# Choosing experts on VectorE: 112 candidate sums for each head in place of 256, in wide operations with one operand in PSUM

## The chip, the cores and the metric

The kernel runs on one core of a Trainium2 chip. The metric is the device time of one execution in microseconds (us), as the median of several runs. A profile of one execution stands beside it.

## The reference, cut to what matters

The reference is a two-part model of two layers each over 256 tokens of width 1024. The change lies in the second part, in the feed-forward of product-key experts (`peer_ffn`), once for each of the two layers. For every token and each of 8 heads it finds the 16 best of 128 keys in each of two halves, adds every value of the one half to every value of the other, and takes the 16 best of these 256 sums. The place of each of the 16 tells which two keys make the expert:

```python
scores = jnp.einsum('thcd,hcnd->thcn', q, sub_keys)
sv, si = lax.top_k(scores, PEER_TOPK)                      # 16 of 128, for two halves
cand_s = (sv[:, :, 0, :, None] + sv[:, :, 1, None, :]).reshape(t, PEER_HEADS, 256)
cand_i = (si[:, :, 0, :, None] * PEER_NKEYS + si[:, :, 1, None, :]).reshape(t, PEER_HEADS, 256)
best_s, best_p = lax.top_k(cand_s, PEER_TOPK)
idx = jnp.take_along_axis(cand_i, best_p, axis=-1)
gate = jax.nn.softmax(best_s, axis=-1)
```

Then the chosen experts' rows of two tables weigh the output: gelu of the token's product with one table, times the gate, times the other.

## The kernel before, in words

The kernel is a row of stages, each a block in which the engines run their own instruction lists and meet through semaphores, with a barrier behind it. The second part runs its stages in a hardware loop over two layers. The stage of the change is `choose_stage`.

In it, 44 weight tiles pass through TensorE: 16 for the queries of the heads' halves (HC), then 28 (EARLY) that hold the first experts' table and have nothing to do with the choice. SyncE loads each tile (L217), ScalarE rounds it to a high part (L255), GpSimd subtracts to get the low part (L262, `weights.low` with `nc.gpsimd`; elsewhere VectorE does this), and TensorE multiplies (L193). The high and low parts have two slots in SBUF. ScalarE copies each query out (L1955) and runs gelu over each of the 28 early results (L1959).

VectorE follows the queries: `best_keys` (L1989 to L2000) finds the 16 best of 128 scores in two rounds, each a MAX8, a FIND_INDEX8 and, in the first, a MATCH_REPLACE8 that takes the eight found away. When the 16 halves are done VectorE goes on alone, while TensorE, ScalarE and GpSimd do the early tiles. Tokens lie on the 128 partitions in two blocks, so there are `pairs` = 16 groups of (block, head). In this order:

- L2027 casts the found indices to float (`half_key`).
- L2031, 16 times, writes the 256 sums of one pair into `k.cand`. Both operands are slices of `half_val` in SBUF, repeated along one axis each.
- `top16` (L2014 to L2024) searches the 256 sums of every pair: 16 MAX8, 16 times FIND_INDEX8 and MATCH_REPLACE8, 16 MAX8, 16 FIND_INDEX8.
- Twice, for the row and for the column of the place: a shift or mask (L2038), a cast (L2039), 16 comparisons with 0 to 15 that make one-hot rows of 16 (L2043), 16 products with the keys (L2048), and one sum over the rows (L2051) into `key_i` or `key_j`.
- L2054 subtracts the largest value, ScalarE takes the exponent (L1977), and VectorE sums, inverts and multiplies (L2057 to L2061).

`s(...)` waits for the instruction it issues; `s.step(...)` doesn't, and `s.settle()` waits for all before. TensorE turns `key_i`, `key_j` and the gates with six transposes (L1944), after ScalarE has finished the early tiles and VectorE the gates. VectorE copies them out (L2065), and `scatter_stage` begins after the barrier. On ScalarE the exponent stands behind the last gelu, and another activation table is loaded between them. PSUM has 8 banks; the stage uses 0 to 3 for products and 4 to 7 for scores. The names `cand`, `half_val` and others are cuts of one tile, so that the profile calls them all `gates`.

Of the kernel before, what the change touches and what calls it, by code (L numbers as in the profile page):

```python
# [22 lines left out]
U32 = mybir.dt.uint32  # L23
ALU = mybir.AluOpType
ACT = mybir.ActivationFunctionType
AX_X = mybir.AxisListType.X

P = 128
# [34 lines left out]
PH, NK, TOPK = 8, 128, 16  # L63
HC = 2 * PH
SLOTS = PH * TOPK
EARLY = 28

RAW, SPLIT = 4, 2
# [1815 lines left out]
def choose_stage(k, l, weights, norm):  # L1884
# [3 lines left out]
    nc, pairs = k.nc, TB * PH  # L1888
    n_tiles, low = HC + EARLY, -3.0e38
    last_turn = n_tiles // RAW - 1  # L1890
    best = lambda half: slice(8 * half, 8 * half + 8)
    with stage(nc, *WEIGHT_SEMS, "keys_in", "kept", "scored", "scores_used", "row_step", "step", "gate_step", "turned",
# [17 lines left out]
        def _(pe):  # L1910
# [31 lines left out]
            for n, x in enumerate((k.key_i, k.key_j, k.gates)):  # L1942
                for b in range(TB):
                    last = nc.tensor.transpose(k.ps[:, n, b * P:(b + 1) * P], x[:, b * SLOTS:(b + 1) * SLOTS], k.const("ident"))  # L1944
            last.then_inc(turned, 1)
# [34 lines left out]
        def _(dve):  # L1980
# [27 lines left out]
            s = Steps(dve, step)  # L2008

            def top16(n, scores, spare, values, index, width):  # L2010

                at = lambda x, r: x[:, r * width:(r + 1) * width]
                for r in range(n):
                    s.step(nc.vector.max(values[:, r, best(0)], at(scores, r)))  # L2014
                s.settle()
                for r in range(n):
                    s.step(nc.vector.max_index(index[:, r, best(0)], values[:, r, best(0)], at(scores, r)))
                    s.step(nc.vector.match_replace(at(spare, r), values[:, r, best(0)], at(scores, r), low))
                s.settle()
                for r in range(n):  # L2020
                    s.step(nc.vector.max(values[:, r, best(1)], at(spare, r)))
                s.settle()
                for r in range(n):
                    s.step(nc.vector.max_index(index[:, r, best(1)], values[:, r, best(1)], at(spare, r)))  # L2024
                s.settle()

            s(nc.vector.tensor_copy(k.half_key[:, :, :], k.half_at[:, :, :]))  # L2027

            for n in range(pairs):
                cand = k.cand[:, n * 256:(n + 1) * 256].rearrange("p (a b) -> p a b", a=TOPK)  # L2030
                s.step(nc.vector.tensor_tensor(cand, k.half_val[:, 2 * n, :].unsqueeze(2).broadcast_to([P, TOPK, TOPK]),  # L2031
                                               k.half_val[:, 2 * n + 1, :].unsqueeze(1).broadcast_to([P, TOPK, TOPK]), ALU.add))
            s.settle()
            top16(pairs, k.cand, k.cand_spare, k.pair_val, k.pair_at, TOPK * TOPK)

            flat_at = k.pair_at[:, :, :].rearrange("p n k -> p (n k)")
            for key, half, op, by in ((k.key_i, 0, ALU.logical_shift_right, 4), (k.key_j, 1, ALU.bitwise_and, TOPK - 1)):
                s(nc.vector.tensor_scalar(k.place_int[:, :], flat_at, by, None, op))  # L2038
                s(nc.vector.tensor_copy(k.place[:, :], k.place_int[:, :]))  # L2039

                for n in range(pairs):
                    hot = k.cand[:, n * 256:(n + 1) * 256].rearrange("p (k a) -> p k a", a=TOPK)
                    s.step(nc.vector.tensor_tensor(hot, k.place[:, n * TOPK:(n + 1) * TOPK].unsqueeze(2).broadcast_to([P, TOPK, TOPK]),  # L2043
                                                   k.const("iota")[:, 0:TOPK].unsqueeze(1).broadcast_to([P, TOPK, TOPK]), ALU.is_equal))
                s.settle()
                for n in range(pairs):
                    hot = k.cand[:, n * 256:(n + 1) * 256].rearrange("p (k a) -> p k a", a=TOPK)
                    s.step(nc.vector.tensor_tensor(hot, hot, k.half_key[:, 2 * n + half, :].unsqueeze(1).broadcast_to([P, TOPK, TOPK]),  # L2048
                                                   ALU.mult))
                s.settle()  # L2050
                s(nc.vector.reduce_sum(key[:, :], k.cand[:, :].rearrange("p (m a) -> p m a", a=TOPK), AX_X))  # L2051

            gates = k.gates[:, :].rearrange("p (n k) -> p n k", k=TOPK)
            nc.vector.tensor_tensor(gates, k.pair_val[:, :, :], k.pair_val[:, :, 0:1].broadcast_to([P, pairs, TOPK]),  # L2054
# [13 lines left out]
def scatter_stage(k):  # L2068

    nc, lot, lots, late = k.nc, 4, 4, NK - EARLY
    turns_all = SEQ // (lots * lot)
# [16 lines left out]
    with stage(nc, "one_hot", "gated", "spread", "copied", "weighted") as (block, one_hot, gated, spread, copied, weighted):  # L2090

        @block.vector
        def _(dve):
# [10 lines left out]
            def weigh_early(i, n):  # L2104
                early = k.early[:, :, bass.ds(token(i, n), lot)]
                dve.wait_ge(copied, i * lots + n + 1)
                nc.vector.tensor_tensor(early, early, k.ps[:, n, :].rearrange("p (t j) -> p j t", t=lot)[:, 0:EARLY, :],
                                        ALU.mult).then_inc(weighted, 1)
# [19 lines left out]
        def _(act):  # L2128
# [7 lines left out]
            def keep(i, n):  # L2136
                act.wait_ge(spread, i * lots + n + 1 + lots)
                nc.scalar.activation(
                    k.dense[:, bass.ds(token(i, n) * late, lot * late)].rearrange("p (t j) -> p t j", t=lot),
                    k.ps[:, n, :].rearrange("p (t j) -> p t j", t=lot)[:, :, EARLY:NK], ACT.Copy).then_inc(copied, 1)  # L2140

# [3 lines left out]
def experts_stage(k, weights, norm):  # L2145

    nc, n_tiles = k.nc, EARLY + 2 * (NK - EARLY)
    first_turn, last_turn = EARLY // RAW, n_tiles // RAW - 1  # L2150
    dense = k.dense[:, :].rearrange("p (t j) -> p t j", j=NK - EARLY)
# [143 lines left out]
def second_block(k, scope, sb):  # L2295

    nc = k.nc
# [5 lines left out]
    hot = Carver(k.ring.rearrange("p s m -> p (s m)"))  # L2303
# [19 lines left out]
    choose = Carver(k.dense)  # L2323
# [3 lines left out]
    k.half_at = choose(TB * HC, TOPK).bitcast(U32)  # L2327
    pairs = TB * PH
    k.pair_val, k.pair_at = choose(pairs, TOPK), choose(pairs, TOPK).bitcast(U32)
    k.place, k.place_int = choose(pairs * TOPK), choose(pairs * TOPK).bitcast(U32)  # L2330
    k.key_i, k.key_j, k.gates, k.gate_sum = choose(TB * SLOTS), choose(TB * SLOTS), choose(TB * SLOTS), choose(pairs)
    k.cand, k.cand_spare = choose(pairs * TOPK * TOPK), choose(pairs * TOPK * TOPK)
    k.y_natural = Carver(k.dense)(TB, D)
# [105 lines left out]
def program(nc, dram, out):  # L2439
# [10 lines left out]
    with ExitStack() as ctx:  # L2450
# [23 lines left out]
        with ExitStack() as scope:  # L2474
            second_block(k, scope, sb)
# [144 lines left out]
```

## Time and profile before

| what | us |
|---|---|
| median of 3 runs | 3794.24 |
| lowest and highest run | 3782.53 and 3801.14 |
| the profiled execution | 3782.04 |
| its span, from the first to the last instruction | 3780.3 |
| its mean granted TensorE clock | 0.926 |
| TensorE busy | 3398.4 (90%) |
| VectorE busy | 2605.4 (69%) |
| ScalarE busy | 1808.1 (48%) |
| GpSimd busy | 267.1 (7%) |

In the profile PE is TensorE, DVE VectorE, ACT ScalarE and POOL GpSimd. A row names the line of the kernel, the operation, what it writes and reads, its shape and its count; in brackets stands the idle time in front of it and who ended it. Spans of instructions of one engine can overlap a little, so that the time from start to start is less than the duration. The stage of the change ends near 1818 us of the span in the first layer and near 3012 us in the second.

### The profile page before, as it was taken

To read this page: it belongs to the slowest core of one execution; us is meant where nothing else is said; L and a number is where in the kernel's file an instruction comes from. 1 tells how busy PE (TensorE), PEld (TensorE's weight loads), DVE (VectorE), ACT (ScalarE), POOL (GpSimd) and SP (SyncE) were. 2 spreads that over 40 slices of the span, in tenths; PEclk is the share of its full clock that TensorE was granted. 3 is DMA by queue.
4 is the path that set the end of the run, shared out by engine and by line. 5 is a ranking of instruction groups with operands and counts; after the bars stand their busy time and mean duration, and the time that the engine had idled before them with its cause. 6 is when DMAs were issued, how large, how long until landed. Compare 5 with 4: busy or idle time off the path is not lost. (4 is left out here: it accounts for less than half of the span.)

```text
span 3780.3 us, 66192 instructions
## 1 busy us (share of the span) xinstructions
PE 3398.4 (90%) x20396; PEld 2933.4 (78%) x20396; DVE 2605.4 (69%) x5277; ACT 1808.1 (48%) x3489; POOL 267.1 (7%) x204
## 2 busy tenths in 40 slices
PE   7999999999898988689589999998679679999999
PEld 5767767777698986489568999997459658999998
DVE  6667767766567756369976777775538997777775
ACT  4543233324465544346655445443435484444454
POOL 0000000000000002038000000000206500000000
PEclk8899989999899988589899999998769899999999
DMA  5125424342154543044046666664114206666664
GB/s 189 37 106 173 164 98 149 125 162 79 49 178 145 173 143 121 1 135 144 0 139 186 185 188 185 187 188 134 65 45 148 87 17 189 188 185 187 188 185 138
DMA packets 138511, 508.87 MB, mean 135 GB/s; under 512 B 15632, under 2 KB 16016, under 8 KB 137360
## 3 DMA queue, kind: packets, MB, share of 16 engines
q1 hardware_dynamic: 137664, 504.56, 41.8%
q10 hardware_dynamic: 720, 2.71, 0.2%
q8 instruction: 69, 1.13, 0.1%
q14 instruction: 58, 0.48, 0.0%
HBM read 506.16 MB, written 1.05 MB: 134 GB/s over the span
## 5 line engine op out<-in xcount | busy, mean ns | idle before, releaser
L255 ACT ACTIVATE split<-ring 128x512 fp32r<-128x512 f32 (+1 forms) x1700 | 1061.9, 628 | 1422.6 <-PE ps L193 1357.3
L262 DVE TENSOR_TENSOR split<-ring,split 128x512 fp32r<-128x512 f32 (+1 forms) x1500 | 1022.8, 687 | 714.9 <-ACT split L255 694.6
L193 PEld LDWEIGHTS ps<-h2T,split 128*128 128x128 f32 x7776 | 969.1, 193 | 29.8 <-DVE h2T L490 14.4
L193 PE MATMUL ps<-h2T,split 128*128 128x256 f32 x7776 | 981.3, 285 | 12.0 <-DVE h2T L490 12.0
L193 PE MATMUL ps<-split,chunk 128*128 128x512 f32 x3072 | 738.7, 392 | 18.9 <-DVE chunk L2255 16.9
L193 PEld LDWEIGHTS ps<-split,chunk 128*128 128x128 f32 x3072 | 566.4, 189 | 130.2 <-DVE chunk L2255 17.3
L193 PE MATMUL ps<-hT,split 128*128 128x512 f32 (+1 forms) x3504 | 643.0, 345 | 15.9 <-DVE hT L492 8.8
L193 PEld LDWEIGHTS ps<-hT,split 128*128 128x128 f32 x3504 | 546.0, 191 | 109.2 <-DVE hT L492 12.8
L262 POOL TENSOR_TENSOR split<-ring,split 128x512 fp32r<-128x512 f32 x200 | 266.9, 1356 | 2713.6 <-ACT split L255 2709.5
L193 PE MATMUL ps<-act_chunk,split 128*128 128x512 f32 (+1 forms) x1056 | 188.6, 340 | 13.6 <-DVE act_chunk L597 13.6
L2123 PE MATMUL ps<-ring 128*128 128x128 f32 x1024 | 150.6, 293 | 49.6 <-DVE ring L2101 49.1
L193 PEld LDWEIGHTS ps<-act_chunk,split 128*128 128x128 f32 x1056 | 163.9, 191 | 35.9 <-DVE act_chunk L597 14.2
L2123 PEld LDWEIGHTS ps<-ring 128*128 128x128 f32 x1024 | 128.0, 196 | 72.7 <-ACT ring L2133 72.7
L2133 ACT ACTIVATE ring<-ring,slot_gate 128x128 f32<-128x128 f32 x384 | 126.1, 391 | 27.7 <-DVE ring L2098 12.1
L2270 DVE TENSOR_TENSOR gated<-gelu,gates 128x256 f32<-128x256 f32 x200 | 123.9, 619 | 2.0 <-ACT gelu L2229 2.0
L2275 DVE TENSOR_TENSOR chunk<-gated,chunk 128x256 fp32r<-128x256 f32 x200 | 85.1, 426 | 6.8
L2098 DVE TENSOR_TENSOR ring<-const_sb,slot_j 128x512 f32<-128x512 f32 x128 | 87.2, 681 | 0.0
L193 PE MATMUL ps<-y_chunk,split 128*128 128x512 f32 (+1 forms) x384 | 72.9, 351 | 13.5 <-DVE y_chunk L597 13.5
L193 PEld LDWEIGHTS ps<-y_chunk,split 128*128 128x128 f32 x384 | 61.5, 197 | 22.6 <-DVE y_chunk L597 14.1
L2229 ACT ACTIVATE gelu<-ps 128x256 f32<-128x256 f32 x200 | 73.2, 366 | 0.0
L2098 DVE TENSOR_TENSOR ring<-const_sb,slot_i 128x384 f32<-128x384 f32 x128 | 70.1, 548 | 2.3 <-PEq L2115 2.3
L193 PE MATMUL ps<-branchT,split 128*128 128x512 f32 (+1 forms) x384 | 68.7, 335 | 0.0
(317 smaller groups left out, 3216.0 us busy)
## 6 DMA issues: line engine op xcount, KB each, us to landing
ring<-peer_uv SPq DMA_DIRECT2D x456, 512.0 KB, 3.5
ring<-w_up SPq DMA_DIRECT2D x88, 512.0 KB, 3.4
ring<-w_choose SPq DMA_DIRECT2D x88, 512.0 KB, 3.6
ring<-w_merge SPq DMA_DIRECT2D x64, 512.0 KB, 3.4
ring<-w_down SPq DMA_DIRECT2D x44, 512.0 KB, 3.2
mix_row_ring<-w_mod SPq DMA_DIRECT2D x40, 512.0 KB, 3.6
ffn_row_ring<-w_mod SPq DMA_DIRECT2D x40, 512.0 KB, 3.4
ring<-w_transposed SPq DMA_DIRECT2D x36, 512.0 KB, 4.4
```

What stands on the lines that cost most here:

```text
L193: ins = nc.tensor.matmul(out, lhsT(a), rhs(b), start=first and n == 0, stop=last and n == len(PASSES) - 1)
L255: self.nc.scalar.activation(self.split[:, s % SPLIT, 0, cols], self.ring[:, s, cols], ACT.Copy).then_inc(self.high_ready, 1)
L262: (ops or self.nc.vector).tensor_tensor(self.split[:, s % SPLIT, 1, cols], self.ring[:, s, cols], self.split[:, s % SPLIT, 0, cols].bitcas ...
L2098: nc.vector.tensor_tensor(hot[:, n * lot:n * lot + many, :], iota[:, 0:many, :], keys, ALU.is_equal).then_inc(one_hot, 1)
L2123: last = nc.tensor.matmul(k.ps[:, n, u * NK:(u + 1) * NK], k.hot_i[:, n * lot + u, :], k.hot_j[:, n * lot + u, :], start=True, stop=True)
L2133: nc.scalar.activation(hot, hot, ACT.Copy, scale=k.slot_gate[:, bass.ds(token(i, n) + u, 1)]).then_inc(gated, 1)
L2229: nc.scalar.activation(k.gelu[:, buf, :], k.ps[:, buf, 0:SEQ], ACT.Gelu_apprx_tanh).then_inc(gelu_done, 1)
L2270: nc.vector.tensor_tensor(k.gated[:, :], k.gelu[:, buf, :], dense[:, :, bass.ds(j - EARLY, 1)].rearrange("p t j -> p (t j)"), ALU.mult).th ...
L2275: nc.vector.tensor_tensor(low, k.gated[:, :], high.bitcast(F32), ALU.subtract).then_inc(weighted, 1)
```

## The change

The two halves are sorted from large to small, so the sum at row a and column b has at least (a+1)(b+1)-1 sums before it that are no smaller. The change keeps rows 0 to 3 with all 16 columns and rows 4 to 15 with 4 columns: 64 + 48 = 112 sums. They are made for all sixteen pairs at once, by two operations, whose second operand was copied into PSUM before. The search runs over 112 values. Its places have two ways of counting, so the decoding computes both with whole-width operations: `place` by a shift of 4 and a mask of 15, `few` by a shift of 2 less 12 and a mask of 3, and adds the difference where the place is 64 or more. The result goes to PSUM. The one-hot rows, the products with the keys (keys in PSUM) and the sums then take one operation each over all sixteen pairs.

```diff
+WIDE_A, FEW_B = 4, 4
+CAND_WIDE, CAND_FEW = WIDE_A * TOPK, (TOPK - WIDE_A) * FEW_B
+CANDS = CAND_WIDE + CAND_FEW
...
-            for n in range(pairs):
-                cand = k.cand[:, n * 256:(n + 1) * 256].rearrange("p (a b) -> p a b", a=TOPK)
-                s.step(nc.vector.tensor_tensor(cand, k.half_val[:, 2 * n, :].unsqueeze(2).broadcast_to([P, TOPK, TOPK]),
-                                               k.half_val[:, 2 * n + 1, :].unsqueeze(1).broadcast_to([P, TOPK, TOPK]), ALU.add))
+            halves = k.half_val.rearrange("p (n h) k -> p n h k", h=2)
+            in_psum = lambda bank: k.ps[:, bank, :].rearrange("p (n k) -> p n k", k=TOPK)
+            s.step(nc.vector.tensor_copy(in_psum(4), k.half_val[:, :, :]))
+            s(nc.vector.tensor_copy(in_psum(5), k.half_key[:, :, :]))
+            halves_psum = in_psum(4).rearrange("p (n h) k -> p n h k", h=2)
+            cand = k.cand[:, 0:pairs * CANDS].rearrange("p (n c) -> p n c", n=pairs)
+            for first, rows_of, cols_of, at in ((0, WIDE_A, TOPK, 0), (WIDE_A, TOPK - WIDE_A, FEW_B, CAND_WIDE)):
+                shape = [P, pairs, rows_of, cols_of]
+                s.step(nc.vector.tensor_tensor(
+                    cand[:, :, at:at + rows_of * cols_of].rearrange("p n (a b) -> p n a b", a=rows_of),
+                    halves[:, :, 0, first:first + rows_of].unsqueeze(3).broadcast_to(shape),
+                    halves_psum[:, :, 1, 0:cols_of].unsqueeze(2).broadcast_to(shape), ALU.add))
             s.settle()
-            top16(pairs, k.cand, k.cand_spare, k.pair_val, k.pair_at, TOPK * TOPK)
+            top16(pairs, k.cand, k.cand_spare, k.pair_val, k.pair_at, CANDS)
 
             flat_at = k.pair_at[:, :, :].rearrange("p n k -> p (n k)")
-            for key, half, op, by in ((k.key_i, 0, ALU.logical_shift_right, 4), (k.key_j, 1, ALU.bitwise_and, TOPK - 1)):
-                s(nc.vector.tensor_scalar(k.place_int[:, :], flat_at, by, None, op))
-                s(nc.vector.tensor_copy(k.place[:, :], k.place_int[:, :]))
...
+            late, few, place = k.late_at, k.place_few, k.place
+            s.step(nc.vector.tensor_scalar(k.place_int[:, 0, :], flat_at, 4, None, ALU.logical_shift_right))
+            s.step(nc.vector.tensor_scalar(k.place_int[:, 1, :], flat_at, TOPK - 1, None, ALU.bitwise_and))
+            s.step(nc.vector.tensor_scalar(k.place_int[:, 2, :], flat_at, 2, None, ALU.logical_shift_right))
+            s.step(nc.vector.tensor_scalar(k.place_int[:, 3, :], flat_at, FEW_B - 1, None, ALU.bitwise_and))
+            s(nc.vector.tensor_copy(k.place_at[:, :], flat_at))
+            s.step(nc.vector.tensor_copy(place[:, :, :], k.place_int[:, 0:2, :]))
+            s.step(nc.vector.tensor_copy(few[:, :, :], k.place_int[:, 2:4, :]))
+            s(nc.vector.tensor_scalar(late[:, :], k.place_at[:, :], float(CAND_WIDE), None, ALU.is_ge))
+            s(nc.vector.tensor_scalar(few[:, 0, :], few[:, 0, :], float(CAND_WIDE // FEW_B - WIDE_A), None, ALU.subtract))
+            s(nc.vector.tensor_tensor(few[:, :, :], few[:, :, :], place[:, :, :], ALU.subtract))
+            s(nc.vector.tensor_tensor(few[:, :, :], few[:, :, :], late[:, :].unsqueeze(1).broadcast_to([P, 2, pairs * TOPK]), ALU.mult))
+            place_psum = k.ps[:, 6, :].rearrange("p (h m) -> p h m", h=2)
+            s(nc.vector.tensor_tensor(place_psum, place[:, :, :], few[:, :, :], ALU.add))
+            hot = k.cand[:, :].rearrange("p (n k a) -> p n k a", n=pairs, k=TOPK)
+            keys = in_psum(5).rearrange("p (n h) k -> p n h k", h=2)
+            flat_hot, shape = k.cand[:, :].rearrange("p (m a) -> p m a", a=TOPK), [P, pairs * TOPK, TOPK]
+            for half, key in enumerate((k.key_i, k.key_j)):
+                s(nc.vector.tensor_tensor(flat_hot, place_psum[:, half, :].unsqueeze(2).broadcast_to(shape),
+                                          k.const("iota")[:, 0:TOPK].unsqueeze(1).broadcast_to(shape), ALU.is_equal))
+                s(nc.vector.tensor_tensor(hot, hot, keys[:, :, half, :].unsqueeze(2).broadcast_to([P, pairs, TOPK, TOPK]), ALU.mult))
+                s(nc.vector.reduce_sum(key[:, :], flat_hot, AX_X))
```

The new `place`, `place_few`, `late_at`, `place_int` and `place_at` are further cuts of the same SBUF tile.

## Rows read from the trace of the kernel before

**Rows 1.** Busy time in stretches of the stage: length, engines (instructions), granted clock, DMA.

```profile
core 0: us, PE busy (x) PEld busy (x) DVE busy (x) ACT busy (x) POOL busy (x), PEclk, DMA share, GB/s
1714.00:1738.00 24.00, 24.00 (x203) 24.00 (x202) 23.93 (x25) 18.37 (x31) 22.44 (x17) 1.00 0.55 167
...
1760.00:1789.00 29.00, 29.00 (x244) 29.00 (x244) 28.86 (x50) 17.22 (x32) 25.81 (x19) 1.00 0.39 120
1789.00:1815.00 26.00, 0.87 (x8) 0.67 (x6) 25.25 (x51) 2.08 (x3) 0.00 (x0) 0.57 0.00 0
...
2983.00:3009.00 26.00, 0.69 (x6) 0.49 (x5) 25.21 (x52) 2.08 (x3) 0.00 (x0) 0.58 0.00 0
```

**Rows 2.** Timeline of TensorE: start us, duration us, what, and the wait before.

```profile
1709.79 80.08 PE L193 MATMUL ps<-h2T,split 128*128 128x256 f32 x666
1815.68 1.51 PE L1944 MATMUL ps<-const_sb,gates 128*128 128x128 f32 x6 [25.81 <-DVE gates L2061]
```

**Rows 3.** Timeline of ScalarE at the stage's end, in both layers.

```profile
1789.91 0.38 ACT L1959 ACTIVATE gates<-ps 128x256 f32<-128x256 f32 x1 [2.49 <-PE ps L193]
1790.31 1.28 ACT L1977 ACT_TABLE_LOAD   x1
1813.92 0.42 ACT L1977 ACTIVATE gates<-gates 128x256 f32<-128x256 f32 x1 [22.32 <-DVE gates L2054]
...
2984.13 1.28 ACT L1977 ACT_TABLE_LOAD   x1
3007.74 0.42 ACT L1977 ACTIVATE gates<-gates 128x256 f32<-128x256 f32 x1 [22.33 <-DVE gates L2054]
```

**Rows 4.** Timeline of VectorE in the first layer, behind the last `best_keys`.

```profile
1714.48 20.90 DVE L2031 TENSOR_TENSOR gates<-gates 128x256 f32<-128x256 f32 x16
1735.41 5.32 DVE L2014 MAX8 gates<-gates 128x8 f32<-128x256 f32 x16
...
1765.33 1.05 DVE L2038 TENSOR_SCALAR gates<-gates 128x256 uint32<-128x256 uint32 x1
1766.42 1.27 DVE L2039 CAST gates<-gates 128x256 f32<-128x256 uint32 x1
1767.72 19.67 DVE L2043 TENSOR_TENSOR gates<-gates,const_sb 128x256 f32<-128x256 f32 x16
1787.42 5.46 DVE L2048 TENSOR_TENSOR gates<-gates 128x256 f32<-128x256 f32 x16
1792.91 4.42 DVE L2051 TENSOR_REDUCE gates<-gates 128x256 f32<-128x4096 f32 x1
1797.37 0.29 DVE L2038 TENSOR_SCALAR gates<-gates 128x256 uint32<-128x256 uint32 x1
...
1798.02 5.46 DVE L2043 TENSOR_TENSOR gates<-gates,const_sb 128x256 f32<-128x256 f32 x16
...
1813.46 0.42 DVE L2054 TENSOR_TENSOR gates<-gates 128x256 f32<-128x256 f32 x1
```

**Rows 5.** Timeline of GpSimd: beside the queries, and beside the candidate sums.

```profile
1670.32 1.29 POOL L262 TENSOR_TENSOR split<-ring,split 128x512 fp32r<-128x512 f32 x1 [0.59 <-ACT split L255]
...
1715.08 22.71 POOL L262 TENSOR_TENSOR split<-ring,split 128x512 fp32r<-128x512 f32 x16 [0.92 <-ACT split L255]
...
1769.80 17.31 POOL L262 TENSOR_TENSOR split<-ring,split 128x512 fp32r<-128x512 f32 x12 [0.92 <-ACT split L255]
```

**Rows 6.** Timeline of VectorE in the second layer's scatter stage, where GpSimd is idle.

```profile
3013.75 0.69 DVE L2098 TENSOR_TENSOR ring<-const_sb,slot_j 128x512 f32<-128x512 f32 x1
...
3017.47 0.27 DVE L2107 TENSOR_TENSOR gates<-gates,ps 128x112 f32<-128x112 f32 x1
```

**Rows 7.** VectorE's groups by line and shape: count, busy us, mean ns of one.

```profile
L1989 DVE MAX8 gates<-ps 128x8 f32<-128x128 f32 x64 | 15.9, 290 | 16.6 <-PE ps L1920 16.3
L1997 DVE MAX8 gates<-gates 128x8 f32<-128x128 f32 x64 | 15.8, 287 | 4.9
...
L2014 DVE MAX8 gates<-gates 128x8 f32<-128x256 f32 x32 | 10.7, 410 | 0.1
```

More of the change, by code:

```diff
@@ L2033, in _ @@
             s.settle()
-            top16(pairs, k.cand, k.cand_spare, k.pair_val, k.pair_at, TOPK * TOPK)
+            top16(pairs, k.cand, k.cand_spare, k.pair_val, k.pair_at, CANDS)
             flat_at = k.pair_at[:, :, :].rearrange("p n k -> p (n k)")
-            for key, half, op, by in ((k.key_i, 0, ALU.logical_shift_right, 4), (k.key_j, 1, ALU.bitwise_and, TOPK - 1)):
-                s(nc.vector.tensor_scalar(k.place_int[:, :], flat_at, by, None, op))
-                s(nc.vector.tensor_copy(k.place[:, :], k.place_int[:, :]))
[L2041 to L2051, printed above, removed]
@@ L2329, in second_block @@
     k.pair_val, k.pair_at = choose(pairs, TOPK), choose(pairs, TOPK).bitcast(U32)
-    k.place, k.place_int = choose(pairs * TOPK), choose(pairs * TOPK).bitcast(U32)
+    k.place, k.place_few, k.late_at = choose(2, pairs * TOPK), choose(2, pairs * TOPK), choose(pairs * TOPK)
+    k.place_int, k.place_at = choose(4, pairs * TOPK).bitcast(U32), choose(pairs * TOPK)
     k.key_i, k.key_j, k.gates, k.gate_sum = choose(TB * SLOTS), choose(TB * SLOTS), choose(TB * SLOTS), choose(pairs)
```

## The prediction

> **What bounds the kernel now.** The change touches one stage, the choice of experts, which runs once in each of two layers, so I read the view by stretches first. While TensorE works on the stage's 44 weight tiles it is busy the whole time at the full granted clock of 1.00, with VectorE busy beside it; then come 26 us (in either layer) in which TensorE does 0.7 to 0.9 us of work, VectorE 25.2, and the granted clock falls to 0.57 [rows 1]. The timeline of TensorE says whose wait that is: its stream of 666 matmuls ends at 1789.9, and its next work, the six transposes of the chosen slots, starts at 1815.68 after 25.81 us idle, released by VectorE's last gate multiplication, L2061 [rows 2]. The timeline of ScalarE shows what lies between: the last gelu copy ends at 1790.3, the load of the exponent's table runs unasked behind it until 1791.6, and then ScalarE waits 22.32 us (22.33 in layer 2) for the gate subtraction L2054 of VectorE [rows 3]. So in the last quarter of the stage VectorE's chain is the bound, and before that TensorE's stream.
>
> VectorE's timeline shows this chain: from 1714.48 to 1813.9 without a gap worth the name [rows 4]. Three things are to be seen there. The candidate sums take 20.90 us for 16, 1.3 us each, and the first 16 comparisons 19.67, while the second 16 comparisons, with the same shape and line, take 5.46, that is 0.34 each. GpSimd tells the two apart: it splits weights from before the slow sums until 1787.1 and has ended before the fast comparisons, and while the slow sums run, its own instructions follow each other at 22.71 / 16 = 1.42 us against 1.29 for one alone [rows 5]. The two engines take turns, and VectorE pays about one GpSimd instruction for each of its own that has both operands in SBUF. The single-operand shift and cast are also slowed, from 0.29 to 1.05 and 1.27 us, but the searches are not.
>
> **The change part by part.** All durations follow one line: 256 elements take 0.42 us [rows 4], 512 take 0.69 [rows 6] and 4096 take 4.42 [rows 4], so 0.15 us and 1.04 ns for each element. The chain of one layer, from 1714.48:
>
> Copies into PSUM. Two copies of 512 elements are added: 2 x 0.69 = 1.4 us. Were the one from SBUF to run at double rate it would be less by some 0.3; each may wait one GpSimd instruction, 1.0 more.
>
> Candidate sums. 16 instructions of 256 go (20.9 us), two wide ones come with 1024 and 768 elements: 1.22 + 0.95 = 2.2 us. No row shows a wide operation with one operand in SBUF and one in PSUM beside a busy GpSimd. The nearest are MAX8, which reads PSUM in 290 ns and SBUF in 287 with GpSimd busy [rows 7], and the product L2107, 112 elements in 0.27 us with one operand in PSUM and an innermost run of four, with GpSimd idle [rows 6]; 0.15 + 112 x 1.04 ns gives the same 0.27. I take the plain rate and no waiting. The other ends are under the rivals.
>
> The search top16. It stays at 16 x 5 = 80 passes, each over 112 in place of 256 values. MAX8 goes from 410 ns at 256 to 287 at 128 [rows 7], 1.0 ns for a value, so 80 x 144 x 1.0 ns = 11.5 us go from the 29.9 between 1735.41 and 1765.33 [rows 4], and 18.4 stay.
>
> The decoding. Two shifts or masks and two casts become twelve instructions: four shifts and masks, one cast of 256, two casts of 512, a comparison, a subtraction, and three tensor-tensor operations of 512. At the undisturbed rate that is 5 x 0.29 for the first kinds, 2 x 0.42 (256 more elements at twice the rate), 2 x 0.29 and 3 x 0.69, in sum 4.9, with the gaps 5.4 us. All twelve have two SBUF operands or are of the kind that rows 4 show slowed, by 0.76 to 0.98 us; GpSimd will be busy then, so I take 1.0 each: 17.4 us. The bound from below is 5.4.
>
> The lookup. 64 narrow operations and two reductions, 19.67 + 5.46 + 4.42 and then 5.46 + 5.46 + 4.42, become four wide operations and the same two reductions, 6 x 4.42 and gaps: 26.7 us against 45.7 with the old decoding steps among them. The gate subtraction costs 0.4 as before.
>
> Sum: 1.4 + 2.2 + 18.4 + 5.4 + 26.7 + 0.5 = 54.6 us without any waiting, 69 us with 12 to 14 waits of 1.0. The chain then ends between 1769 and 1783 and no longer at 1813.9. I take 1781 or so: 30 us less of VectorE's time and more per layer.
>
> What counts of it. ScalarE can start the exponent at 1791.6 at the earliest, behind the last gelu copy (which waits for TensorE's last tile) and the table load [rows 3]. VectorE will be ready 9 to 22 us before. So of VectorE's 30 to 45 us only the 22.32 and 22.33 us of ScalarE's wait come off the path, 44.65 us in all; what is late next is TensorE's own stream. Behind the exponent everything keeps its length. TensorE's stream is not shortened, since it is at 100% already. The restarted transposes took 1.51 us at the low clock [rows 2]; with a gap of 3.5 us in place of 25.8 the clock may stay up, worth at most half of it, 0.8 us a layer, which I leave out. No DMA, no other queue and no wait of another engine is touched, except GpSimd: its splits have 2.9 us of pace for 2 x 1.29 us of work, and about a dozen short holds more or fewer cost TensorE nothing, as the 16 holds of the candidate sums cost it nothing now (its share stays 24.00 of 24.00 [rows 1]).
>
> The profiled execution took 3782.04 us with a span of 3780.3. Less 44.65 that gives 3737.4; the median of the three timed runs lies 12.2 us above this execution, so I predict 3749.6, say 3750 us, 1.2% less.
>
> The Trainium skill, "SBUF — State Buffer", section "Who interferes with whom", states that a VectorE instruction with at most one SBUF input, outside the two-port modes, does not contend with GpSimd, while one with two SBUF inputs does, and that the loser blocks for the whole instruction. By that the six wide operations hold nobody and the time is the one above; were the operand's place in PSUM of no use, it would be that of the first rival. The trace agrees for the two-operand case (1.3 against 0.34 us) and shows nothing of the mixed one.
>
> **The rivals.** First: the wide operations keep GpSimd out. For it speaks that two-operand work and GpSimd's do exclude each other here; against it, that the PSUM reader MAX8 doesn't show it. Price: the wide operations with two inputs hold 2.2 + 4 x 4.42 = 19.9 us a layer. From 1714.5 to 1787 GpSimd does about 52 instructions x 1.29 = 67 us of work in 72.6, so 5.5 are free and TensorE's weights, and its stream, come up to 14.4 us later. Saved: 22.3 - 14.4 = 7.9 a layer, 16 in all: 3778 us.
>
> Second: the wide patterns (four dimensions, repeats at stride 0, PSUM) stream at two cycles for an element. 18,176 elements x 1.04 ns = 18.9 us more, the chain ends between 1788 and 1802, and up to 10.4 us a layer of the gain go: 3750 to 3770 us. Rows 4 speak against it: the narrow ones have the same repeats and run at one cycle.
>
> Third, on the other side: the same place at four cycles for an element. 57 us more, the chain ends between 1826 and 1840, 12 to 26 us a layer after 1813.9: 3818 to 3846 us. It decides from 2.6 to 3.4 cycles, where the chain is as long as before (31 to 45 us over 18.9 us a cycle). Only the missing row for wide mixed operations speaks for it.
>
> Fourth: the change shortens VectorE, but another delay appears in the gap, say TensorE's queue needing instructions after a short pause that the long one hid; a few us a layer, about 3760.
>
> **How the numbers follow.** Chances: forecast 0.84, first rival 0.08, second 0.04, third 0.02, fourth 0.02. The forecast's own spread is that of the runs, -12 to +7 us around their median, and I stretch it for the median of another set: 3730 to 3770. The range is 3730 to 3772, which holds the second and fourth too. Half a per cent, 19 us, is about what a measurement here can tell from nothing: faster (under 3775) 0.90, within 0.08, slower 0.02.
>
> **What would show it.** Right: ScalarE's wait before the exponent is gone (under 1 us), TensorE's gap before the transposes is 3 to 4 us, the wide sums take 1.2 and 0.95 us and the wide lookups 4.4, and GpSimd runs on at 1.4 us beside them. Wrong: lookups of 8 us or more; a hole of 4 us in GpSimd's splitting with TensorE idle beside it (first rival); a remaining wait for L2054's successor; or a longer scatter stage.

## The result, and the profile after

The changed kernel takes 3738.95 us as the median of 4 runs (3732.3 to 3753.37), the kernel before 3788.41 (3782.53 to 3801.14; a fourth run, 3782.59, joined the three that the prediction had): a ratio of 0.9872, with a 95% interval of 0.9849 to 0.9896. The profiled execution took 3737.64 us with a span of 3735.9, that is 44.4 us less span than before, where the prediction's sum had 44.65.

The timeline of VectorE in the changed kernel, first layer, answers to [rows 4]:

```profile
1714.17 0.52 DVE L2030 CAST gates<-gates 128x512 f32<-128x512 uint32 x1
1714.73 0.69 DVE L2034 COPY ps<-gates 128x512 f32<-128x512 f32 x1
1715.33 0.68 DVE L2035 COPY ps<-gates 128x512 f32<-128x512 f32 x1
1716.05 2.08 DVE L2040 TENSOR_TENSOR gates<-gates,ps 128x1024 f32<-128x1024 f32 x2
1718.17 2.92 DVE L2017 MAX8 gates<-gates 128x8 f32<-128x112 f32 x16
...
1736.08 0.85 DVE L2049 TENSOR_SCALAR gates<-gates 128x256 uint32<-128x256 uint32 x1
1736.86 1.38 DVE L2050 TENSOR_SCALAR gates<-gates 128x256 uint32<-128x256 uint32 x1
1738.16 0.28 DVE L2051 TENSOR_SCALAR gates<-gates 128x256 uint32<-128x256 uint32 x1
...
1748.89 1.69 DVE L2061 TENSOR_TENSOR ps<-gates 128x512 f32<-128x512 f32 x1
1750.61 4.42 DVE L2066 TENSOR_TENSOR gates<-ps,const_sb 128x4096 f32<-128x4096 f32 x1
1755.07 4.42 DVE L2068 TENSOR_TENSOR gates<-gates,ps 128x4096 f32<-128x4096 f32 x1
...
1777.34 0.94 DVE L2072 TENSOR_TENSOR gates<-gates 128x256 f32<-128x256 f32 x1
1792.31 0.42 DVE L2075 TENSOR_REDUCE gates<-gates 128x16 f32<-128x256 f32 x1 [14.02 <-ACT gates L1980]
```

The chain ends at 1778.3, where before it ended at 1813.9, and now VectorE waits: 14.02 us for ScalarE's exponent. The four wide lookup operations, which have one operand in PSUM, take 4.42 us each while GpSimd splits weights beside them. The decoding in front of them, which reads SBUF alone, still pays for GpSimd: 1.38 us for a mask that takes 0.28 when it is free.

GpSimd's own timeline, beside the decoding and beside the lookup:

```profile
1738.38 8.21 POOL L265 TENSOR_TENSOR split<-ring,split 128x512 fp32r<-128x512 f32 x6 [0.29 <-ACT split L258]
...
1761.41 7.72 POOL L265 TENSOR_TENSOR split<-ring,split 128x512 fp32r<-128x512 f32 x6 [0.33 <-ACT split L258]
```

Beside the wide lookup its instructions follow each other at 7.72 / 6 = 1.29 us, the time of one alone: there neither engine holds the other.

ScalarE and TensorE, answering to [rows 3] and [rows 2]:

```profile
1790.16 0.38 ACT L1962 ACTIVATE gates<-ps 128x256 f32<-128x256 f32 x1 [2.49 <-PE ps L196]
1790.56 1.28 ACT L1980 ACT_TABLE_LOAD   x1
1791.86 0.42 ACT L1980 ACTIVATE gates<-gates 128x256 f32<-128x256 f32 x1
```

```profile
1709.25 80.88 PE L196 MATMUL ps<-h2T,split 128*128 128x256 f32 x672
1793.62 1.51 PE L1947 MATMUL ps<-const_sb,gates 128*128 128x128 f32 x6 [3.49 <-DVE gates L2079]
```

The 22.32 us of ScalarE's wait are gone, the exponent follows its table load at once, and TensorE's gap is 3.49 us for 25.81. TensorE's stream keeps its old length: 672 matmuls in 80.88 us. Before it was the same; the 666 in 80.08 of [rows 2] are the part of this stream that fell into the stretch asked for.

The profiled executions of all the kernels here differ by up to 25 us ahead of the stage (the cast of the found indices starts between 1704 and 1729 us); the cause of that stays open. A cleaner measure than the whole time is therefore the stretch from the cast of the found indices (L2027, now L2030) to the first of the six transposes, read from the timelines of VectorE and TensorE. It was 1815.68 - 1713.92 = 101.76 us before and is 1793.62 - 1714.17 = 79.45 us after, 22.31 less; in the second layer 101.77 and 79.46.

### The profile page after: what moved, and what is told of

Same layout as the page of the kernel before. It is cut to its first block and busy times, and to the rows that moved or that the text cites. A ratio compares the mean times of both kernels' runs of the same rounds, so it can differ in the third digit from the quotient of the medians.

```text
span 3735.9 us, 66064 instructions
## 1 busy us (share of the span) xinstructions
PE 3401.3 (91%) x20396; PEld 2938.4 (79%) x20396; DVE 2532.1 (68%) x5149; ACT 1807.8 (48%) x3489; POOL 262.8 (7%) x204
## 5 line engine op out<-in xcount | busy, mean ns | idle before, releaser
L196 PEld LDWEIGHTS ps<-h2T,split 128*128 128x128 f32 x7776 | 968.6, 193 | 29.9 <-DVE h2T L493 14.4
L196 PE MATMUL ps<-h2T,split 128*128 128x256 f32 x7776 | 980.8, 285 | 12.1 <-DVE h2T L493 12.1
L2151 ACT ACTIVATE ring<-ring,slot_gate 128x128 f32<-128x128 f32 x384 | 126.1, 391 | 28.0 <-DVE ring L2116 12.1
L2247 ACT ACTIVATE gelu<-ps 128x256 f32<-128x256 f32 x200 | 73.2, 366 | 0.0
```

Of the source, the lines that this page charges most:

```text
L196: ins = nc.tensor.matmul(out, lhsT(a), rhs(b), start=first and n == 0, stop=last and n == len(PASSES) - 1)
L2151: nc.scalar.activation(hot, hot, ACT.Copy, scale=k.slot_gate[:, bass.ds(token(i, n) + u, 1)]).then_inc(gated, 1)
L2247: nc.scalar.activation(k.gelu[:, buf, :], k.ps[:, buf, 0:SEQ], ACT.Gelu_apprx_tanh).then_inc(gelu_done, 1)
```

## The experiments

Each kernel was timed beside the kernel before on the same chip, but not all on one chip: e1 to e4 make one set, e5 to e8 another, e9 and e10 a third. Between sets the ratios compare, not the times. The table gives the stretch in the first layer; the second layer agrees within 0.3 us.

| run | cast to transposes, us | time, us (median) | ratio to before, 95% interval |
|---|---|---|---|
| before | 101.76 | 3788.41 | |
| the change | 79.45 | 3738.95 | 0.9872 (0.9849 to 0.9896) |
| e1 wide, all in SBUF | 96.75 | 3773.38 | 0.9957 (0.9942 to 0.9971) |
| e2 wide, PSUM, 256 sums | 79.46 | 3747.28 | 0.9886 (0.9850 to 0.9923) |
| e3 before, one operand in PSUM | 79.45 | 3750.89 | 0.9894 (0.9865 to 0.9923) |
| e4 112 sums, narrow, SBUF | 99.46 | 3779.74 | 0.9987 (0.9972 to 1.0001) |
| e5 8.9 us more of VectorE | 79.44 | 3741.08 | 0.9868 (0.9836 to 0.9900) |
| e6 26.7 us more of VectorE | 92.12 | 3762.64 | 0.9926 (0.9897 to 0.9955) |
| e7 early tail | 75.79 | 3731.72 | 0.9858 (0.9831 to 0.9885) |
| e8 the change again | 79.44 | 3739.91 | 0.9878 (0.9855 to 0.9902) |
| e9 e2 with the early tail | 75.80 | 3731.46 | 0.9856 (0.9830 to 0.9882) |
| e10 sums in quarters | 105.44 | 3801.55 (1 run) | |

**e1: wide operations without PSUM.** This asks whether the place of the operand or the width makes the gain.

```diff
-            s.step(nc.vector.tensor_copy(in_psum(4), k.half_val[:, :, :]))
-            s(nc.vector.tensor_copy(in_psum(5), k.half_key[:, :, :]))
...
-                    halves_psum[:, :, 1, 0:cols_of].unsqueeze(2).broadcast_to(shape), ALU.add))
+                    halves[:, :, 1, 0:cols_of].unsqueeze(2).broadcast_to(shape), ALU.add))
...
-            s(nc.vector.tensor_tensor(place_psum, place[:, :, :], few[:, :, :], ALU.add))
+            s(nc.vector.tensor_tensor(place[:, :, :], place[:, :, :], few[:, :, :], ALU.add))
...
-            keys = in_psum(5).rearrange("p (n h) k -> p n h k", h=2)
+            keys = k.half_key.rearrange("p (n h) k -> p n h k", h=2)
...
-                s(nc.vector.tensor_tensor(flat_hot, place_psum[:, half, :].unsqueeze(2).broadcast_to(shape),
+                s(nc.vector.tensor_tensor(flat_hot, place[:, half, :].unsqueeze(2).broadcast_to(shape),
```

> The change with no operand in PSUM: the two wide sums, the four wide lookup operations and the decoding all read SBUF alone, and the two copies into PSUM are gone. Theory (two SBUF operands and a GpSimd instruction exclude each other for the whole instruction): each of the six wide operations first waits up to 1.3 us for GpSimd, and then holds GpSimd for its 1.2, 0.95 or 4.4 us. The chain of VectorE ends some 5 to 8 us later than in the changed kernel, still before ScalarE is ready, but GpSimd's splitting shows holes of 4.4 us, TensorE waits beside them, and its stream ends 10 to 14 us later in each layer: 20 to 28 us more than the changed kernel, 16 to 25 less than the kernel before. Rival (only VectorE pays, as the narrow operations seemed to show): GpSimd runs on, and the time is that of the changed kernel within 5 us.

The timeline of TensorE in this run shows where the time goes:

```profile
1710.16 44.88 PE L196 MATMUL ps<-h2T,split 128*128 128x256 f32 x372
1758.09 1.70 PE L196 MATMUL ps<-h2T,split 128*128 128x256 f32 x12 [3.05 <-POOL split L265]
1763.50 7.51 PE L196 MATMUL ps<-h2T,split 128*128 128x256 f32 x48 [3.71 <-POOL split L265]
1772.63 1.69 PE L196 MATMUL ps<-h2T,split 128*128 128x256 f32 x12 [1.62 <-POOL split L265]
1778.03 30.32 PE L196 MATMUL ps<-h2T,split 128*128 128x256 f32 x228 [3.72 <-POOL split L265]
```

VectorE and the clock beside it, from the timeline and the stretches (the columns are those of [rows 1]):

```profile
1751.52 5.40 DVE L2061 TENSOR_TENSOR gates<-gates,const_sb 128x4096 f32<-128x4096 f32 x1
...
1781.34 0.64 DVE L2067 TENSOR_TENSOR gates<-gates 128x256 f32<-128x256 f32 x1
...
1810.53 0.42 DVE L2070 TENSOR_REDUCE gates<-gates 128x16 f32<-128x256 f32 x1 [28.55 <-ACT gates L1980]
```

```profile
1755.00:1785.00 30.00, 17.91 (x108) 17.26 (x108) 26.77 (x7) 9.33 (x15) 28.85 (x12) 0.83 0.30 87
```

VectorE loses 0.2 to 1.0 us on each wide lookup operation (5.40 for 4.42 on the first), its chain ends 66.9 us after the cast for 64.1 in the changed kernel, still long before ScalarE is ready, and it waits 28.55 us. The damage is on the other side. GpSimd is held out for whole operations (its longest split lasts 5.45 us, in the changed kernel 1.75), and TensorE waits for it four times, 12.1 us in all. The stream takes 98.2 us, 17.3 more than in the changed kernel; the 5.2 us beyond the waits are slower matmuls (48 take 7.51 us, where the pace of the changed kernel gives 5.8), at a granted clock of 0.83 in the mean of this stretch. With the 17.0 us of the second layer that is 34.3 us, more than the 20 to 28 expected; the ratios to before, 0.9957 and 0.9872, are some 32 us apart. So the theory holds in kind, and the first rival of the prediction would have been the outcome without PSUM. Its price of 14.4 us a layer was too high for the waits alone (12.1) and left out the clock (5.2).

**e2: wide and in PSUM, but all 256 sums.**

```diff
-            for first, rows_of, cols_of, at in ((0, WIDE_A, TOPK, 0), (WIDE_A, TOPK - WIDE_A, FEW_B, CAND_WIDE)):
...
+            s(nc.vector.tensor_tensor(cand, halves[:, :, 0, :].unsqueeze(3).broadcast_to(full),
+                                      halves_psum[:, :, 1, :].unsqueeze(2).broadcast_to(full), ALU.add))
...
             s.step(nc.vector.tensor_scalar(k.place_int[:, 0, :], flat_at, 4, None, ALU.logical_shift_right))
...
+            s(nc.vector.tensor_scalar(k.place_int[:, 1, :], flat_at, TOPK - 1, None, ALU.bitwise_and))
+            s(nc.vector.tensor_copy(place_psum, k.place_int[:, 0:2, :]))
```

> The wide operations with an operand in PSUM, but all 256 sums and the old, simple decoding (one shift, one mask, one cast). Theory (what counts is only that the chain ends before ScalarE is ready, 14 us after it in the changed kernel): sums 4.4 us for 2.1, search 29.9 for 17.9, decoding about 3 for 14.5, so the chain ends within 3 us of where the changed kernel's ends, ScalarE does not wait, and the time is that of the changed kernel: 44 us less than before. Rival (the 112 sums bring part of the gain): some us per layer more than the changed kernel, at 11.5 us of search a layer up to 23.

```profile
1719.95 4.42 DVE L2039 TENSOR_TENSOR gates<-gates,ps 128x4096 f32<-128x4096 f32 x1
1724.40 5.33 DVE L2017 MAX8 gates<-gates 128x8 f32<-128x256 f32 x16
...
1784.05 0.78 DVE L2058 TENSOR_TENSOR gates<-gates 128x256 f32<-128x256 f32 x1
1796.20 0.42 DVE L2061 TENSOR_REDUCE gates<-gates 128x16 f32<-128x256 f32 x1 [11.38 <-ACT gates L1980]
```

In this timeline of VectorE the chain ends 66.8 us after the cast of 1718.06, in the changed kernel 64.1, and 11.38 us of waiting are left. The stretch is that of the change to 0.01 us. The 112 sums bring nothing on the path: the search saves 12 us and the sums 2.3, the decoding gives back 11.5 (14.5 against 3.0), and the some 2.7 us that are left fall into VectorE's wait.

**e3: the kernel before, with one operand in PSUM.** Still pair by pair, all 256 sums.

```diff
+            s.step(nc.vector.tensor_copy(in_psum(4), k.half_val[:, :, :]))
+            s(nc.vector.tensor_copy(in_psum(5), k.half_key[:, :, :]))
...
-                                               k.half_val[:, 2 * n + 1, :].unsqueeze(1).broadcast_to([P, TOPK, TOPK]), ALU.add))
+                                               in_psum(4)[:, 2 * n + 1, :].unsqueeze(1).broadcast_to([P, TOPK, TOPK]), ALU.add))
...
-                s(nc.vector.tensor_copy(k.place[:, :], k.place_int[:, :]))
+                s(nc.vector.tensor_copy(k.ps[:, 6, 0:pairs * TOPK], k.place_int[:, :]))
```

(and the places and keys are read from there in the lookup)

> The kernel before with nothing changed but the place of one operand: second half values, keys and places are copied to PSUM, all 256 sums, pair by pair. Theory (waiting for GpSimd was 30 of the 99 us): sums and first comparisons take 5.5 us each for 20.9 and 19.7, the chain takes about 72 us, ends near 1786, 5 us before ScalarE is ready, and the whole gain of 44 us is there. Rival (number of instructions and width count): 16 narrow operations still take over 5.5 us each group, part of ScalarE's wait stays, and the gain is under 35 us.

```profile
1724.30 5.39 DVE L2034 TENSOR_TENSOR gates<-gates,ps 128x256 f32<-128x256 f32 x16
...
1761.35 5.39 DVE L2046 TENSOR_TENSOR gates<-ps,const_sb 128x256 f32<-128x256 f32 x16
...
1800.56 0.42 DVE L2060 TENSOR_REDUCE gates<-gates 128x16 f32<-128x256 f32 x1 [6.80 <-ACT gates L1977]
```

```profile
1723.58 7.72 POOL L262 TENSOR_TENSOR split<-ring,split 128x512 fp32r<-128x512 f32 x6 [0.92 <-ACT split L255]
```

These timelines, of VectorE and of GpSimd, have the sharpest comparison of the study. The same 16 operations take 5.39 us for 20.90 and 5.39 for 19.67 [rows 4], with GpSimd splitting beside them as before, by moving one of two operands. VectorE keeps 6.80 us of waiting, and the stretch is 79.45 us: the whole gain of the change. The whole time alone would not tell it from the rival, which had under 35 us: the median is 35.8 us below before, with an interval of 29 to 51.

**e4: the 112 sums alone**, narrow and from SBUF.

```diff
+                for n in range(pairs):
+                    s.step(nc.vector.tensor_tensor(
+                        cand[:, n, at:at + rows_of * cols_of].rearrange("p (a b) -> p a b", a=rows_of),
+                        halves[:, n, 0, first:first + rows_of].unsqueeze(2).broadcast_to(shape),
+                        halves[:, n, 1, 0:cols_of].unsqueeze(1).broadcast_to(shape), ALU.add))
```

(with the decoding of the change, its result in SBUF, and the lookup of the kernel before)

> The 112 sums alone: built pair by pair from SBUF in 32 operations, decoded as in the change, looked up pair by pair from SBUF. Theory: 32 sums that each wait for one GpSimd instruction take 43 us for 20.9, the search 18 for 29.9, the decoding 14 to 17 for 3; at about 1790 GpSimd has ended and the lookup runs undisturbed in 31 us. The chain ends near 1820, 6 to 8 us later than before: 12 to 16 us slower than the kernel before. Rival (less search is worth its 11.5 us): some us faster than before.

```profile
1729.27 10.84 DVE L2037 TENSOR_TENSOR gates<-gates 128x64 f32<-128x64 f32 x32
...
1769.99 22.93 DVE L2061 TENSOR_TENSOR gates<-gates,const_sb 128x256 f32<-128x256 f32 x16
1792.96 13.06 DVE L2066 TENSOR_TENSOR gates<-gates 128x256 f32<-128x256 f32 x16
```

The expectation missed the sign: the stretch is 2.3 us shorter a layer and not 6 to 8 longer. The 32 sums took 10.84 us and not 43. Grouped by shape in the same stretch, it is the second half of them that paid nothing (busy us, mean ns of one, idle time):

```profile
L2037 DVE TENSOR_TENSOR gates<-gates 128x64 f32<-128x64 f32 x16 | 8.9, 633 | 0.0
L2037 DVE TENSOR_TENSOR gates<-gates 128x48 f32<-128x48 f32 x16 | 2.0, 196 | 0.0
```

So "one wait for each operation" is not the rule. The search took the 18 us expected and the decoding 11.9, less than its 14 to 17. The lookup did not run undisturbed in 31 us: it began while GpSimd was still splitting, its first comparisons and products took 22.93 and 13.06 us for 5.46 when free, and it took 56.0 us in all for 45.7 before. That eats most of what sums and search saved, and the chain ended 97.7 us after the cast, 100.0 before. The time is 0.1% below before, within what can be told from nothing.

**e10: the sums in quarters**, to see why e4 missed: the kernel before, each sum cut into four operations of 64 elements.

```diff
-                s.step(nc.vector.tensor_tensor(cand, k.half_val[:, 2 * n, :].unsqueeze(2).broadcast_to([P, TOPK, TOPK]),
-                                               k.half_val[:, 2 * n + 1, :].unsqueeze(1).broadcast_to([P, TOPK, TOPK]), ALU.add))
+                for q in range(0, TOPK, 4):
+                    s.step(nc.vector.tensor_tensor(cand[:, q:q + 4, :], k.half_val[:, 2 * n, q:q + 4].unsqueeze(2).broadcast_to([P, 4, TOPK]),
+                                                   k.half_val[:, 2 * n + 1, :].unsqueeze(1).broadcast_to([P, 4, TOPK]), ALU.add))
```

> The kernel before with each candidate sum cut into four operations of 64 elements, still from SBUF: 64 for 16. Theory after the run with few narrow sums (VectorE pays one GpSimd instruction for each turn that GpSimd gets, and fits two or more short operations between two of them): 64 operations / 2.3 for each turn x 1.42 us = 40 us at most, and less where GpSimd pauses, so the sums take 25 to 40 us for 20.9 and the stage is 4 to 19 us longer in each layer. Rival (each operation with two SBUF operands waits for one GpSimd instruction, as in the kernel before): 64 x 1.3 = 83 us, so that it runs on beyond GpSimd's end.

VectorE, GpSimd (its instructions in that stretch: shortest, median and longest in ns), TensorE, and two stretches with the columns of [rows 1]:

```profile
1725.66 15.44 DVE L2032 TENSOR_TENSOR gates<-gates 128x64 f32<-128x64 f32 x64
```

```profile
L262 POOL TENSOR_TENSOR split<-ring,split x8: 1275/1296/7327, 1726.3 to 1742.2; 128x512 fp32r<-128x512 f32 x8
```

```profile
1742.28 65.44 PE L193 MATMUL ps<-h2T,split 128*128 128x256 f32 x528 [4.58 <-POOL split L262]
```

```profile
1725.60:1734.90 9.30, 9.30 (x80) 9.30 (x80) 9.27 (x20) 6.51 (x13) 7.63 (x7) 1.00 0.50 143
1734.90:1741.20 6.30, 2.79 (x24) 2.59 (x22) 6.26 (x47) 3.67 (x6) 6.30 (x1) 0.87 0.37 126
```

Both the expectation (25 to 40 us) and its rival (83) missed: 64 operations take 15.44 us. The two stretches show two regimes. Up to 1734.9 GpSimd splits without much pause, and VectorE gets 20 operations through in 9.3 us. At 1734 GpSimd pauses for 0.92 us, as it does now and then for ScalarE, and from there VectorE's short operations follow each other without letting GpSimd in: about 47 in 6.3 us, while one single GpSimd instruction lasts 7.33 us and not 1.29. TensorE waits 4.58 us for it. In e4 the second half of the sums looks the same on a smaller scale: behind a pause of 0.92 us one GpSimd instruction lasts 2.76 us.

The sums are 5.5 us shorter than before, and yet the transposes come 3.7 us later in the first layer and 3.5 in the second. The lookup shows why:

```profile
1772.79 20.75 DVE L2044 TENSOR_TENSOR gates<-gates,const_sb 128x256 f32<-128x256 f32 x16
1793.57 14.17 DVE L2049 TENSOR_TENSOR gates<-gates 128x256 f32<-128x256 f32 x16
```

GpSimd, once held up, splits until 79.7 us after the cast, before until 73.2, and so the first products too run beside it: 14.17 us for 5.46.

**e5 and e6: more work for VectorE.** The changed kernel with two (the edit shown), and with six, more reductions ahead of the gate subtraction; they do not change the output.

```diff
+            for _ in range(2):
+                s(nc.vector.reduce_sum(k.place_at[:, :], flat_hot, AX_X))
```

> The changed kernel with two more sums over 4096 elements (the same reduction, written to a tile that nobody reads then) before the gate subtraction: 8.9 us more of VectorE in each layer. Theory (14 us of VectorE's time are idle behind the chain in each layer): nothing moves, the time is that of the changed kernel, and VectorE's wait for the exponent falls from 14.0 to about 5 us. Rival (something else behind the chain depends on it): up to 18 us more.

> The same with six such sums, 26.7 us more of VectorE in each layer. Theory: 13.6 us of it are hidden, 13.1 us a layer come onto the path, and ScalarE waits about that long before the exponent: 26 us more than the changed kernel, 18 less than the kernel before. Rival as before: 53 us more.

With 8.9 us more nothing moves: the stretch is 79.44 us. With 26.7 us more the stretch grows by 12.67 us, and ScalarE shows the wait again, in its timeline:

```profile
1816.71 0.42 ACT L1980 ACTIVATE gates<-gates 128x256 f32<-128x256 f32 x1 [12.69 <-DVE gates L2075]
```

So 14.0 us a layer are free on VectorE behind the chain, which is what the profile of the changed kernel shows as its wait.

**e7, e8 and e9: the tail.** What is late next is the tail behind the last gelu: table load, exponent, three short operations, transposes. e7 takes the exponent two tiles earlier, into the time in which VectorE waits, and sends the transposes to banks 4 to 6, so that they need not wait for the last gelu (VectorE copies them out from there); e8 is the changed kernel again; e9 is e7's tail on e2.

```diff
                 keep_early(last_turn, s)
-            act.wait_ge(gate_step, 1)
-            nc.scalar.activation(k.gates[:, :], k.gates[:, :], ACT.Exp).then_inc(gate_step, 1)
+                if s == 1:
+                    act.wait_ge(gate_step, 1)
+                    nc.scalar.activation(k.gates[:, :], k.gates[:, :], ACT.Exp).then_inc(gate_step, 1)
...
-            pe.wait_ge(kept, n_tiles + RAW)
             pe.wait_ge(gate_step, 5)
...
-                    last = nc.tensor.transpose(k.ps[:, n, b * P:(b + 1) * P], x[:, b * SLOTS:(b + 1) * SLOTS], k.const("ident"))
+                    last = nc.tensor.transpose(k.ps[:, RAW + n, b * P:(b + 1) * P], x[:, b * SLOTS:(b + 1) * SLOTS], k.const("ident"))
```

> The changed kernel with its tail moved into the idle time: ScalarE takes the exponent behind the second gelu of the last four tiles and no longer behind the last, the six transposes go to banks 4 to 6 and no longer wait for the last gelu. Theory: the exponent runs near 1786, TensorE's transposes follow its last tile without a gap at the full clock, and the stage ends 3.5 to 4.5 us earlier in each layer: 7 to 9 us less than the changed kernel. Rival (the two more loads of ScalarE's table delay the last gelu copies, or the barrier waits for something else): no difference from the changed kernel.

> The changed kernel itself, beside the others on the same chip: 1.1 to 1.3% less than the kernel before, the wait of ScalarE before the exponent gone in both layers.

> All 256 sums and the simple decoding in wide operations with one operand in PSUM, and the early tail. Theory: the chain ends 66.8 us after the cast of the indices as in the run with 256 wide sums, ScalarE takes the exponent 72 us after it in the early tail, so nothing waits: the transposes start 75.8 us after the cast as in the changed kernel with the early tail, 79.45 in the changed kernel, and the time is 50 to 54 us less than before. Rival (the longer chain meets the earlier exponent): the exponent waits, and up to 4 us a layer are lost.

TensorE in e7:

```profile
1783.79 1.96 PE L196 MATMUL ps<-h2T,split 128*128 128x256 f32 x15
1785.59 0.82 PE L1946 MATMUL ps<-const_sb,gates 128*128 128x128 f32 x6
1790.25 2.07 PE L2141 MATMUL ps<-ring 128*128 128x128 f32 x8 [3.84 <-DVE ring L2119]
```

The stretches of the six transposes, in the changed kernel and in e7 (columns of [rows 1]):

```profile
1793.62:1795.13 1.51, 1.51 (x6) 1.11 (x6) 0.00 (x0) 0.00 (x0) 0.00 (x0) 0.50 0.00 0
1785.59:1786.41 0.82, 0.82 (x8) 0.58 (x6) 0.00 (x0) 0.39 (x1) 0.00 (x0) 1.00 0.00 0
```

In e7 the transposes follow the last tile without a gap and take 0.82 us for 1.51: the granted clock is 1.00 in them, where it is 0.50 behind the pause of 3.49 us in the changed kernel. From the cast (1709.80) to the first matmul of the scatter stage (1790.25) e7 takes 80.45 us, e8 84.77: 4.3 us a layer. The medians agree, 8.2 us less than e8 on the same chip, though the intervals of the two ratios overlap, so that the whole time alone would not show it. e9 gives the same stretch and the same time with fewer instructions than the change.

## Why the prediction was right

**Who waits for whom.** Right, and to a tenth: ScalarE's wait went from 22.32 us to none and the stretch shrank by 22.31. TensorE's stream kept its 80.88 us, as forecast. The step that decided the number was to price the change by that wait and not by the 30 to 45 us that VectorE saves; e5 shows the remainder to be worth nothing, e6 that it comes back once 14 us are used up.

**The chain, term by term** (predicted; measured in the first layer): copies 1.4; 1.3. Sums 2.2; 2.1. Search 18.4; 17.9. Decoding 5.4 to 17.4; 14.5, for twelve instructions of which two escaped. Lookup 26.7; 26.7. Gate subtraction 0.4; 0.94, beside a GpSimd that still splits, where before it had ended. End at 1781; 1778.3. The waits in the decoding came to 9.1 us and not 12. The two that escaped, 0.28 us each from 1738.16 on, began in or at the end of a pause of GpSimd, which waited 0.29 us for ScalarE until 1738.38. None of this reached the time, as VectorE had 14 us to spare. One reading was loose without harm: VectorE's chain bounds 26 us, and the stage takes 166 from its first matmul at 1651.9, so that this is nearer a sixth than "the last quarter".

**The waits for GpSimd.** For operations of 256 elements and more the prediction's reading holds in the main: beside a busy GpSimd each costs VectorE up to about one GpSimd instruction, 1.0 to 1.1 us in most. As a general rule it was too simple, as e4 and e10 show, but nothing in the change hung on it. That an operand in PSUM takes VectorE out of this contest, the open point, was confirmed by e3 and by its opposite, e1. The Trainium skill, "SBUF — State Buffer", section "Who interferes with whom", states this rule, and the trace agrees: 5.39 us for 20.90. It also says that the loser is held for the whole instruction; e10 has a GpSimd instruction of 7.33 us beside some 47 of VectorE, so here the hold lasted over many short ones in a row.

**The rivals.** The first did not happen, but e1 shows that its mechanism exists and is dearer than its price, 17.3 us a layer for 14.4: 12.1 of waits, and 5.2 of matmuls at a lower granted clock. The second and the third fell with the 4.42 us of each wide operation, the plain rate of the prediction's line (0.15 us and 1.04 ns for each element). The fourth: no new delay behind the gap; the transposes still take 1.51 us, at a granted clock of 0.50, behind a pause of 3.5 us as behind one of 25.8, and the possible 0.8 us did not come.

**The time.** The profiled execution came to 3737.64 us, the sum had 3737.4. That the whole time agrees to 0.2 us is luck, since runs of the changed kernel spread from 3732 to 3753 us and the executions differ ahead of the stage; what the prediction got right by its own reasons is the stretch. The predicted 3750 was 11 us above the median. It added the 12.2 us by which the median of the three runs stood above their profiled execution, and that distance was mostly chance: with the fourth run it is 6.4 us for the kernel before, and for the changed kernel it is 1.3.

**Which part of the change did it.** The place of one operand alone (e3) gives all of it. Width without PSUM (e1) gives less than a quarter, 5.0 of 22.3 us a layer. The 112 sums with their decoding alone (e4) give 2.3 us, and on top of the wide operations nothing (e2).

## What to carry to other kernels

Price a faster engine by the wait of the next engine that ends, and then ask what is late next. When VectorE and GpSimd work at the same time, look for two-operand VectorE instructions that take several times as long as the same ones without GpSimd (here 1.3 us for 0.34), and move one operand to PSUM before anything is widened: in e1 the wide instructions with both operands in SBUF hurt GpSimd, and TensorE, which waits for it, more than VectorE. Read such effects from a stretch of the stage; here it repeats to 0.02 us between kernels of equal length while whole times spread by 20.

## What the hardware showed that was not expected

- Short VectorE operations in a row kept GpSimd out: one instruction that takes 1.29 us alone lasted 7.33 us (e10), though each VectorE operation is 0.2 us. In both layers it began behind a pause of GpSimd; why such a run of operations starts there and not earlier is not shown.
- Four waits of TensorE of 1.6 to 3.7 us (12.1 in all) cost another 5.2 us in slower matmuls, at a granted clock of 0.83 in the mean (e1).
- Of four shifts and masks of the changed kernel, issued without a wait between them, the first two took 0.85 and 1.38 us and the other two 0.28 each; those two fell on a pause of GpSimd of 0.29 us. Two casts and a comparison a little later, also without a wait between them, took 1.41, 1.52 and 1.38 us: a row of short operations does not always get through together.
